# A hybrid decoder layer on eight cores: RMSNorm sums taken one row block at a time inside the output projection, and the first modulation units moved ahead of the first input tiles

## What is computed

```python
mod = jax.nn.silu(c) @ w_ada + b_ada
sh1, sc1, g1, sh2, sc2, g2 = split(mod, 6)
h  = _rmsnorm(x, norm1_g) * (1.0 + sc1) + sh1
proj = h @ w_in            # conv branch, q, k, v, two gates
...
x  = x + g1 * (mixed @ w_mix_out)
h2 = _rmsnorm(x, norm2_g) * (1.0 + sc2) + sh2
a, val = jnp.split(h2 @ w_up, 2, axis=-1)
x  = x + g2 * ((gelu(conv(a)) * val) @ w_down)
y  = _rmsnorm(x, final_g)
```

## Time and profile before

| | us |
|---|---|
| median of two timed runs | 1627.9 (1623.78 to 1632.02) |
| profiled execution | 1618.12 |
| its span on the slowest core (core 1) | 1616.6 |
| spans of the eight cores | 1602.3 to 1616.6 |
| PE busy | 1331.7 |
| DVE, ACT, POOL busy | 689.4, 522.7, 96.1 |

### The profile page before, as it was taken

The page is one execution under the profiler, slowest core; times in us unless marked ns, Lnnn a source line. Parts: engine busy times, 40 slices in busy tenths (PEclk is TensorE's granted clock), DMA queues, the critical chain, the costliest instruction groups (busy, mean ns, idle before and its releaser), DMA issues.

```text
span 1616.6 us, 28006 instructions; the slowest of 8 cores (1602.3 to 1616.6 us)
## 1 busy us (share of the span) xinstructions
PE 1331.7 (82%) x10262; PEld 799.8 (49%) x10262; DVE 689.4 (43%) x1584; ACT 522.7 (32%) x922; POOL 96.1 (6%) x184
## 2 busy tenths in 40 slices
PE   1359889878899997988997999987498899588695
PEld 1225555444565655555564565544375455244353
DVE  0123453124688432445224788323115433576612
ACT  0142443113433533344213433423114411322203
POOL 0000000000001000000000001000100000000000
PEclk9669999999999999999999999998669999799896
DMA  6884336884366664433563567752814565255551
GB/s 124 166 155 77 54 66 116 148 149 72 66 105 104 153 131 154 96 53 70 97 98 54 79 104 107 148 112 91 139 27 79 94 113 92 45 96 94 99 96 65
DMA packets 36133, 161.25 MB, mean 100 GB/s; under 512 B 4344, under 2 KB 7288, under 8 KB 29248
## 3 DMA queue, kind: packets, MB, share of 16 engines
q0 software_dynamic: 27840, 130.59, 47.5%
q1 hardware_dynamic: 8160, 28.88, 6.1%
HBM read 280.07 MB, written 13.89 MB: 182 GB/s over the span
## 4 chain that ended last, share of the span: by engine, by line
PE 64%; DVE 11%; DMA 10%; ACT 9%; issue 5%; DVEq 0%; ACTq 0%; POOL 0%; SPq 0%; POOLq 0%
PE ps L396 43%; PE ps L1197 9%; DMA ring<-wmg_t 3%; PE ps L732 2%; ACT pT L702 2%; DVE C_sb L1039 2%; DMA kcT<-ckT 2%; DVE B_sb L1042 2%; DMA ring<-wada_t 2%; PE ps L806 2%; DVE pT L705 1%; PE ps L695 1%; DVE tmp L360 1%; DMA xl<-xin 1%; ACT hT L364 1%
## 5 line engine op out<-in xcount | busy, mean ns | idle before, releaser
L396 PE MATMUL ps<-hT,ring 128*128 128x512 bf16 (+2 forms) x4608 | 772.4, 324 | 50.5 <-DMA ring<-wmg_t 15.6
L396 PEld LDWEIGHTS ps<-hT,ring 128*128 128x128 bf16 x4608 | 418.8, 100 | 364.0 <-issue 96.8
L396 PE MATMUL ps<-arena,ring 128*128 128x512 bf16 (+2 forms) x1152 | 185.5, 317 | 0.0
L1197 PE MATMUL ps<-arena,ring 128*128 128x512 bf16 (+2 forms) x1056 | 165.2, 317 | 0.0
L396 PEld LDWEIGHTS ps<-arena,ring 128*128 128x128 bf16 x1152 | 105.3, 98 | 73.3 <-issue 0.6
L1045 ACT ACTIVATE ge<-B_sb 128x512 bf16<-128x512 bf16 (+2 forms) x132 | 66.7, 505 | 223.0 <-DVE B_sb L1042 217.4
L1197 PEld LDWEIGHTS ps<-arena,ring 128*128 128x128 bf16 x1056 | 95.6, 98 | 67.1 <-issue 1.6
L384 DVE SCALAR_TENSOR_TENSOR xT<-ps,modT,xT 128x512 f32<-128x512 f32 (+1 forms) x80 | 50.9, 643 | 115.5 <-PE ps L1197 89.4
L958 DVE TENSOR_TENSOR t<-ps,sga 128x512 bf16<-128x512 f32 (+2 forms) x48 | 25.7, 536 | 160.6 <-PE ps L396 159.8
L702 ACT ACTIVATE pT<-ps 128x1024 bf16<-128x1024 f32 (+1 forms) x68 | 64.1, 943 | 48.7 <-PE ps L695 46.4
L954 ACT ACTIVATE sga<-ps 128x512 bf16<-128x512 f32 (+2 forms) x48 | 22.7, 473 | 173.3 <-PE ps L396 169.2
(11 more groups left out here) (159 smaller groups left out, 1143.3 us busy)
## 6 DMA issues: line engine op xcount, KB each, us to landing
ring<-wup_t POOLq DMA_DIRECT2D x66, 512.0 KB, 6.0
ring<-wmg_t POOLq DMA_DIRECT2D x24, 1024.0 KB, 9.7
ring<-wcv_t POOLq DMA_DIRECT2D x24, 768.0 KB, 7.1
ring<-wdn_t POOLq DMA_DIRECT2D x24, 704.0 KB, 7.6
xl<-xin SPq DMA_DIRECT2D x27, 512.0 KB, 4.7
ring<-wada_t POOLq DMA_DIRECT2D x12, 1024.0 KB, 10.4
y<-xs SPq DMA_DIRECT2D x17, 512.0 KB
ring<-wq_t POOLq DMA_DIRECT2D x6, 1024.0 KB, 9.1
```

What stands on the lines that cost most here:

```text
L396: P.op("pe", lambda e, kc=kc, l_=l_, r2_=r2_, b=b, n=n: e.matmul(ps[:, b, 0:n], lhsT=l_, rhs=r2_, start=(kc == 0), stop=(kc == 7)), r=[wke ...
L1197: P.op("pe", lambda e, kc=kc, g0=g0, n=n, b=b, ld_=ld_: e.matmul(ps[:, b, 0:n], lhsT=ld_, rhs=AR[:, kc, g0:g0 + n], start=(kc == 0), stop= ...
```

## The change

`norm_stats` and `norm_B` can be told a bank; then the eight matmuls of ones are left out of them. In the mix stage each block's addition is followed at once by its own square on ACT and its own matmul of ones on PE, into bank 7 for group 0 and bank 6 for group 1. These two banks are kept from `alloc` during the stage. At the start, three of the four modulation units stand ahead of the tiles, the fourth between the third and the fourth tile.

```diff
         def alloc():
             b = state["bank"]
+            while b in state.get("excl", ()):
+                b = (b + 1) % 8
             state["bank"] = (b + 1) % 8
...
-        def norm_stats(ch, gi):
+        def norm_stats(ch, gi, bank=None):
...
-            b = alloc()
-            for kc in range(8):
+            b = alloc() if bank is None else bank
+            for kc in range(8 if bank is None else 0):
...
-        phase_B(0, CHUNKS[0])
-        ada_quarter(0)
+        for uu in range(3):
+            ada_unit(0, uu)
+        phase_B(0, CHUNKS[0], tiles=[0, 1, 2])
+        ada_unit(0, 3)
         mod_scale(8, 48)
+        phase_B(0, CHUNKS[0], tiles=[3, 4, 5])
         norm_mod(0, CHUNKS[0], 8, 0)
...
+            state["excl"] = (6, 7)
             for gi, (g0, n, kind) in enumerate(groups):
+                sbk = 7 - (gi % 2)
                 for j in range(8):
...
                     resid_add(b, n, j, g0, gi, kind, 16)
+                    P.op("act", lambda e, j=j, g0=g0, n=n: e.activation(out=hT[:, j, g0:g0 + n], in_=xT[:, j, g0:g0 + n], func=AF.Square),
+                         r=["xT:%d:%d" % (j, gi)], w=["hT:%d:%d" % (j, gi)])
+                    P.op("pe", lambda e, j=j, g0=g0, n=n, sbk=sbk: e.matmul(ps[:, sbk, 0:n], lhsT=ones_b[:], rhs=hT[:, j, g0:g0 + n],
+                                                                           start=(j == 0), stop=(j == 7)),
+                         r=["ones_b", "hT:%d:%d" % (j, gi)], w=[PS(sbk)])
                     if gi > 0 and j == 3:
-                        norm_B(ch, gi - 1, 32, 24)
-                norm_A(ch, gi)
+                        norm_B(ch, gi - 1, 32, 24, bank=7 - ((gi - 1) % 2))
...
-            norm_B(ch, len(groups) - 1, 32, 24)
+            norm_B(ch, len(groups) - 1, 32, 24, bank=7 - ((len(groups) - 1) % 2))
+            state["excl"] = ()
```

More of the change, by code:

```diff
@@ L351, in norm_stats, with norm_B @@
             P.op("act", lambda e, n=n: e.activation(out=rstd[:, 0:n], in_=rs[:, 0:n], func=AF.Exp, scale=-0.5), r=["rs"], w=["rstd"])
-        def norm_B(ch, gi, s_idx, sh_idx):
+        def norm_B(ch, gi, s_idx, sh_idx, bank=None):
             g0, n, kind = ch["groups"][gi]
@@ L356, in norm_B @@
             xk_ = ["xT:%d:%d" % (kc, gi) for kc in range(8)]
-            norm_stats(ch, gi)
+            norm_stats(ch, gi, bank)
             for kc in range(8):
```

## The result

The changed kernel takes 1705.19 us in the median of 11 runs, the kernel before 1621.8 us in 10 runs on the same chip. The ratio is 1.0515, with a 95% interval of 1.0492 to 1.0539: 5.2% slower.

The account below looks back on a forecast made before the run. PE, by far the busiest engine, was taken to bound the kernel. The terms 50 + 14 + 7 + 26 - 13 = +84 us gave 1702 or 1712 us, so the forecast was 1705 us, range 1668 to 1742.

Parts of the forecast that it names:

- the chain: Mix stage: projection, addition, square and matmul of ones follow one another; 3.82 us per 512-column block instead of 1.73.
- the open clock: Mix stage, 512-column blocks and first four 256-column blocks: uncertain PE clock loss, 0 to 52 us, taken as +26.
- the start: Start of the program: earlier weight loads let the q projection begin earlier, -13 us.
- the banks: Mix stage: two banks kept out leave six, and projections need one at a time; nothing priced.
- signs of being wrong: Group 0 waits well under 1.7 us, clock takes one side only, or first q matmul not earlier.
- Group 0: Mix stage, 512-column blocks: PE waits for addition and square, 2.09 us more per block, 24 blocks, +50.2 us.
- Group 1: Mix stage, 256-column blocks (128 in last chunk): added latencies and `norm_B` wait, +5.6 us per full chunk, +14 together.
- the certain part of the clock: Mix stage, group 1, blocks five to eight: half clock after the long fifth-block wait, +7 us.
- half of the 52 us: Mix stage: choice between full clock, cost 0, and half clock, 52 us; taken as +26 us.
- rival (1): Mix stage: clock holds in group 0 and group 1's first four blocks; +58, 1676 to 1686 us; chance 0.20.
- Rival (3): Start of the program: bound by bandwidth, gains 5 us or nothing; +92 to +97, 1710 to 1725 us; chance 0.08.
- Rival (4): Mix stage: PE work before each matmul of ones saves about 5 us a chunk, start 15; 1595 us; chance 0.02.

Follow-up runs that it names:

- lag2: Kernel before with the change's mix stage, but each matmul of ones issued two blocks later, old start; 1626.52 us, ratio 1.0041.
- double_g1: Changed mix stage with the old start, but group 1's projections computed twice into the same bank; 1720.51 us.
- start_hold: Changed start with the old mix stage, but tables and q's weights held until the sixth tile is in `xT`; 1624.15 us.
- start_four: Kernel before with three modulation units, six tiles in four buffers, then the fourth unit; old mix stage; 1611.1 us, ratio 0.9947.

## Why the prediction was right, and where it was not

The total was right, 1705 against 1705.19, and so was the mechanism that makes most of it, the chain in the mix stage. But three terms were not right, and their errors cancel: by the means of the cores -20 (the open clock), +15 (the start) and +5 (the banks); 84 by the sum, 86.6 measured. That the total came out so close is luck. Two of the prediction's own signs of being wrong came: the first q matmul is not earlier (106.0 us against 103.6 in the mean), and in group 0 the clock took one side only.

- **Group 0, +50.2 us: right.** The block takes 3.83 us, by sum 3.82; the wait is 41.5 / 24 = 1.73 us, as forecast. 24 x (3.83 - 1.73) = 50.4. `lag2` shows that it is the order on PE and nothing else.
- **Group 1, +14, with the certain part of the clock, +7: right.** From the fifth block's projection to the sixth's it was 437.50 - 426.88 = 10.62 us, by sum 10.7. With 27.3 and 2.8 for the clock, group 1 of chunk 0 should take 30.1 us; it took 447.56 - 414.41 = 33.15. The difference is the open clock in blocks two to four, 3 x (3.33 - 2.37) = 2.9. (The prediction's 10.7 takes 0.2 off a sum of 10.9 without a reason; 10.62 was measured.)
- **The clock, open part, +26 taken: wrong by 20.** The stages grew by 77.2 us, and 50.2 + 14 + 7 = 71.2, which leaves 6. The step that failed is the choice of half of the 52 us, from rows where PE was busy 72% of the time and the clock 0.84. In group 0 PE worked 55% of the time, less than there, and the clock stayed at 1.00: rival (1) was right for group 0. In group 1 it was wrong. There the clock did fall, after one to three blocks in 12 of 16 places in chunks 0 and 1. That agrees with the rule of the Trainium skill that the prediction weighed ("TensorE: Matmul & The Clock Gate", section "A second HAM failure mode: psum-queue depth-cycling"), and group 0 does not: idle times of 1.73 us between groups of matmuls, 24 of them on each core, cost no clock. What the forecast lacked is shown by `double_g1`: behind 1.03 us of projection a wait of 1.25 us mostly cost the clock, behind 1.91 us it did not.
- **The start, -13: wrong by 15.** The order came out as drawn, with POOL's loads at 41.72 and 17.0 us from the sums to the q projection (18.5 forecast). The step that failed is the tile load of 6.4 us: I took it for tiles that now stand beside the fourth unit's weights, the tables and q's weights, 4.5 MB. At 14.5 us each, the third tile came at 58.75, not 51, and the sums at 93.08, not 72. `start_hold` shows the cause: with the tables and q's weights held, 3.5 MB, the tile takes 6.6 us and the sums come at 68.87. Rival (3) came nearest by its number, but not by its mechanism, that the bytes ahead of q's weights set the start: these had landed some 30 us before they were needed, and PE waited for the tiles that shared the engines with them. `start_four` gains 7.4 us at the q projection, more than the 5 that this rival allows. Transfers that slow each other are what "Key Constraints" in "Trainium Kernel Development and Optimization" of the Trainium skill has the ground for: all queues share 16 DMA engines. The share of 1.04 between 50 and 105.80 agrees.
- **The banks, priced at nothing: wrong by 5.** I had asked whether six banks are enough during the stage; they are (`lag2` keeps the two out as well, and a block of group 0 takes 1.94 us there with no wait). I had not asked where the counter stands afterwards, and the interleaved stage of chunk 2 met it.
- **Rival (4)** had the mechanism that makes such a change pay, other work ahead of each matmul of ones, but its size was off: about 5 us in all three chunks together, not 5 in each, because the long wait is `norm_B`'s. The 15 us at the start were 9.4 even with four buffers.

## What to carry to other kernels

A small matmul that depends on the work just issued belongs some blocks later in PE's order (two were enough here); directly behind its own block it turns three parallel engines into a chain, and the cost is the length of the whole chain less the block's own matmuls, per block. A transfer that is issued earlier is paid for by those beside it, so take the load time of a transfer from a stretch as full as the one it will stand in, and look for who waits next. When buffers are handed out in turn, an edit that takes a different number of them moves every later user: compare stages that the edit doesn't touch.

## What was not expected of the hardware

- The granted clock stayed at 1.00 through 30.5 us in which PE waited 1.73 us in every 3.83, and fell within one block of 2.45 us in which it waited 1.25 (core 3, chunk 0; over the cores in chunks 0 and 1 after one to three such blocks in 12 of 16 places, and in 4 not within them). With the same 1.25 us wait in blocks of 3.28 us it stayed at 1.00 through all four, on all cores in chunks 0 and 1.
- A tile load of 512 KB takes 6.4 to 6.6 us when it is issued ahead of the tables and q's weights and 14.5 beside them. Two loads of 1 MB took 57.8 us in the median beside the cache copies and 31.5 without them.
